# Two triangular inverses under way at once in a chunked recurrence

## The chip, the cores and the metric

The kernel runs on one core of a Trainium2 chip. The metric is the device time of one execution in microseconds (us), the median of three runs. Lower is better.

## The reference, cut to what matters

The reference is two transformer blocks over 1024 tokens of width 1024, all in float32. The change touches one part of the second block's first layer, the RWKV-7 time mix: 12 heads of 64 channels, with a state of 64 x 64 per head that is carried from token to token.

```python
def step(state, inp):
    r_t, w_t, k_t, v_t, kk_t, a_t = inp
    sa = jnp.einsum('bhvk,bhk->bhv', state, -kk_t)
    state = (state * w_t[:, :, None, :]
             + sa[..., None] * (kk_t * a_t)[:, :, None, :]
             + v_t[..., None] * k_t[:, :, None, :])
    y_t = jnp.einsum('bhvk,bhk->bhv', state, r_t)
    return state, y_t
```

## The kernel before, in words

Everything ahead of the recurrence and behind it (the projections, the attentions, the feed-forward) is one long list of steps, each of which issues its instructions on the engines. The recurrence is one step of that list, the class `Rwkv`, between two joins at which all engines wait for each other.

The 1024 tokens are cut into 16 chunks of 64 (`NCH`, `CH`). Inside a chunk the token-by-token update is replaced by matrix products of 64 x 64 per head and by the inverse of a unit lower triangular 64 x 64 matrix per head. The 12 heads lie as 6 pairs; a product for all heads (`heads`, L2281 and on) is 12 matmuls, one per head, and its result fills one PSUM bank, which one instruction of 128 x 384 then reads. A float32 matmul is two instructions in the trace, a float16 one is one.

The work of a chunk is cut into five parts, each a Python generator for every engine, which issues a few instructions between two `yield`s:

- L (`low_rank_*`, 4 steps, for two chunks at a time, so at every second chunk): the decay and rate projections; PE multiplies, DVE adds a bias, ACT takes tanh, and DVE scales the rate (L2321).
- E (`elementwise_*`, 4 steps): step 1 is DVE's decay (L2380) and its running sum, a scan (L2382), and ACT's two exponentials of it (L2361, L2364); step 2 is DVE's three products for the keys and POOL's two behind them (L2347, L2349); step 3 is DVE's L2395, L2396, L2399 and POOL's L2352; step 4 is a PE sum and DVE's bonus (L2403).
- P (`products_*`, 4 steps): step 1 is PE's three products (two of them 128 wide), DVE's masks of them (L2448 to L2460), ACT's cast to float16 (L2493) and POOL's copies and masks; steps 2 to 4 each turn one operand on PE and copy it out of PSUM on ACT (L2499).
- I (`inverse_*`, 12 steps): the inverse by doubling. For each of five levels one step for w (PE product in float16, DVE mask L2538), then one for x (two PE products, DVE additions L2541 and L2543 into `x16` and `xt16`). Step 11 is a refinement in float32: ACT casts `xt16` to `z` (L2560), PE multiplies, DVE subtracts (L2547). Step 12 multiplies once more and adds (L2552).
- S (`state_*`, 4 steps): the state. PE product, ACT copy `rhs` (L2604); PE product, ACT copy `g` (L2607); PE product of the addition; PE product of the output, ACT copy (L2611), DVE's state addition and decay (L2621, L2623).

Each engine runs its instructions strictly in the order in which they were issued and waits for the others by semaphores. That order is set by `order()`, a text of letters written by hand. `run_parts` goes through it on every engine alike: each letter advances that part's generator by a step. In the kernel before, during the states S of chunk m the letters mean: P and I of chunk m+1, E and L of chunk m+2. All 12 steps of a chunk's inverse fall inside the one turn of the loop. There is one set of buffers for the inverse (`low`, `z`, `zi`, `x16`, `xt16`, `w16`, `l16`), and it uses banks 4 (w and the refinement), 5 (x) and 6 (xt); bank 7 serves L, E and the turned operands; banks 0 to 3 serve P, S and half of L.

Of the kernel before, what the change touches and what calls it, by code (L numbers as in the profile page):

```python
# [2171 lines left out]
class Rwkv(Step):  # L2172
# [4 lines left out]
    def __init__(self, k, rkv, lora, rooms):  # L2177
# [17 lines left out]
        self.low, self.z, self.zi = buf(), buf(), buf()  # L2195
        self.x16, self.xt16, self.w16, self.l16 = (buf(BT, CH, dtype=F16) for _ in range(4))
# [20 lines left out]
    def order(self):  # L2217

        out = [("L", 0)] * 4 + [("E", 0)] * 4
        out += [("P", 0)] * 4 + [("I", 0)] * 12 + [("E", 1)] * 4  # L2220
        for m in range(NCH):
            text = ("P L IP L IP L IP L I E I S E I I E S I E I S I I S I" if m % 2 == 0 else
                    "P IP IP IP E I I E I S E I S I E I S I I S I")
            text = "S S S S" if m == NCH - 1 else "P IP IP IP I S I I S I I S I I S I" if m == NCH - 2 else text
            chunk = {"P": m + 1, "I": m + 1, "S": m, "E": m + 2, "L": m + 2}
            count = {c: text.count(c) for c in "PIESL"}
            out += [(c, chunk[c]) for c in text.replace(" ", "")]
            if m < NCH - 1:
# [81 lines left out]

    def low_rank_dve(self, dve, m):
        k, s = self.k, self.s
        for dst, to, bias in (("tw", self.tw, k.vec["a_w0_2"]), ("ta", self.ta, k.vec["a_a0_2"])):
            for half, b in ((0, 7), (1, 0 if dst == "tw" else 1)):
# [55 lines left out]
    def elementwise_dve(self, dve, m):  # L2370
# [32 lines left out]
        dve.scalar_tensor_tensor(vC, self.bank(7), 64.0, self.vc, ALU.mult, ALU.mult).then_inc(*s.bonus.up(m))  # L2403
        yield

    def elementwise_pe(self, pe, m):
        k, s = self.k, self.s
        yield
        yield
        yield  # L2410
        pe.wait_ge(*self.freed(7))
        pe.wait_ge(*s.e_rk.at(m))
        pe.matmul(self.bank(7), k.block64, self.rk.rearrange("p a b -> p (a b)"), start=True, stop=True).then_inc(*s.e_sum.up(m))
        k.free[7] = ("bonus", m)
        yield

    def products_pe(self, pe, m):
# [7 lines left out]
        pe.wait_ge(*self.freed(4))  # L2425
        self.heads(pe, 4, BT, CH, [(self.ar_e[:, :, 0, :], self.bb)]).then_inc(*s.p_low.up(m))
        k.free[4] = ("low", m)
# [6 lines left out]
        for n, src in enumerate((self.vc, self.kb, self.bb)):  # L2434
            if n == 0:
                pe.wait_ge(*s.e_vc.at(m))
            pe.wait_ge(*self.freed(7))
            self.heads(pe, 7, BT, CH, [(src, over_pairs(k.eye))]).then_inc(*s.p_turn.up((m, n)))
            k.free[7] = ("turned_bkv", (m, n))
            yield  # L2440

    def products_dve(self, dve, m):
# [8 lines left out]
        dve.tensor_tensor(self.low, self.bank(4), over_pairs(k.low), ALU.mult).then_inc(*s.low.up(m))  # L2451
        dve.wait_ge(*s.low.at(m))
        if m:
            dve.wait_ge(*s.inv_z.at(m - 1))
        dve.tensor_tensor(self.z, self.low, over_pairs(k.level[0]), ALU.mult).then_inc(*s.step_dve.up(("z", m)))
        dve.wait_ge(*s.step_dve.at(("z", m)))
        dve.tensor_tensor(self.x16, self.z, over_pairs(k.eye), ALU.add).then_inc(*s.inv_x.up((m, 0)))
# [8 lines left out]
    def products_pool(self, pool, m):  # L2466
# [10 lines left out]
        if m:  # L2477
            pool.wait_ge(*s.inv.at(m - 1))
        pool.tensor_tensor(self.zi, self.lr[i][:, :, 0:CH], over_pairs(k.level0t), ALU.mult).then_inc(*s.step_pool.up(("zi", m)))
        pool.wait_ge(*s.step_pool.at(("zi", m)))  # L2480
        pool.tensor_tensor(self.xt16, self.zi, over_pairs(k.eye), ALU.add).then_inc(*s.inv_xt0.up(m))
# [5 lines left out]
    def products_act(self, act, m):  # L2487
# [3 lines left out]
        if m:  # L2491
            act.wait_ge(*s.inv.at(m - 1))
        act.copy(self.l16, self.lr[i][:, :, 0:CH]).then_inc(*s.inv_l.up(m))  # L2493
# [3 lines left out]
        for n, dst in enumerate((self.vt[i], self.kt[i], self.bt[i])):  # L2497
            act.wait_ge(*s.p_turn.at((m, n)))
            act.copy(dst, self.bank(7)).then_inc(*s.turned_bkv.up((m, n)))  # L2499
            yield  # L2500

    def inverse_pe(self, pe, m):
        k, s = self.k, self.s
        for lev in range(1, 6):
# [3 lines left out]
            pe.wait_ge(*self.freed(4))  # L2508
            self.heads(pe, 4, BT, CH, [(self.l16, self.x16)]).then_inc(*s.i_w.up((m, lev)))
            k.free[4] = ("inv_w", (m, lev))  # L2510
            yield
            pe.wait_ge(*self.freed(5))
            pe.wait_ge(*self.freed(6))
# [17 lines left out]
        k.free[5] = ("inv", m)
        yield

    def inverse_dve(self, dve, m):
        k, s = self.k, self.s
        for lev in range(1, 6):
            dve.wait_ge(*s.i_w.at((m, lev)))
            dve.tensor_tensor(self.w16, self.bank(4), over_pairs(k.level[lev]), ALU.mult).then_inc(*s.inv_w.up((m, lev)))  # L2538
            yield
            dve.wait_ge(*s.i_x.at((m, lev)))  # L2540
            dve.tensor_tensor(self.x16, self.x16, self.bank(5), ALU.add).then_inc(*s.inv_x.up((m, lev)))  # L2541
            dve.wait_ge(*s.i_xt.at((m, lev)))
            dve.tensor_tensor(self.xt16, self.xt16, self.bank(6), ALU.add).then_inc(*s.inv_xt.up((m, lev)))  # L2543
# [3 lines left out]
        dve.tensor_tensor(self.r16, self.bank(4), self.zi, ALU.subtract).then_inc(*s.inv_rest.up(m))  # L2547
# [4 lines left out]
        dve.tensor_tensor(self.xt[m % 2], self.z, self.bank(5), ALU.add).then_inc(*s.inv.up(m))  # L2552
        yield

    def inverse_act(self, act, m):
        s = self.s
# [3 lines left out]
        act.copy(self.z, self.xt16).then_inc(*s.inv_z.up(m))  # L2560
# [3 lines left out]
    def inverse_pool(self, pool, m):  # L2564
        s = self.s
# [3 lines left out]
        pool.tensor_tensor(self.zi, self.xt16, over_pairs(self.k.eye), ALU.subtract).then_inc(*s.inv_zi.up(m))  # L2569
# [536 lines left out]
def layer_a(k):  # L3106
# [29 lines left out]
    rwkv = Rwkv(k, (r, key, v), lora, ((k.XH, k.CONST), (F + 6144, F + 8192)))  # L3136
# [3 lines left out]
    yield from [Join(k), RwkvSetup(k, rwkv), KeyNorms(k, key, rwkv.sqs, rwkv.rs12), Join(k), Reset(k, rwkv.reset), rwkv, end]  # L3140
    stored = [(f"dma_stage{j}", main[j - 2].id) for j in range(2)]
# [217 lines left out]
```

## Time and profile before

| what | us |
|---|---|
| median of three runs (3339.84 to 3344.09) | 3340.28 |
| the profiled execution | 3336.7 |
| its span in the profile | 3334.5 |
| recurrence in the span, first heads product to last | 1943.4 to 2415.7 |
| mean granted TensorE clock, share of full | 0.936 |

The page's busy shares over the whole span are PE 86%, DVE 51%, ACT 30% and POOL 21%. They average over stages with quite different limits, so for this change the reader has to look at the recurrence alone, which is a seventh of the span. The profiled execution's own time is 2.2 us above its span. A row of the timeline gives the start of an instruction, or of a run of like ones, its duration, and in brackets how long the engine was idle before it and which instruction released it. Instructions of DVE that follow each other without a wait overlap at their ends: 128 x 384 elements last 0.55 us but start 0.47 us apart.

### The profile page before, as it was taken

To read this page: it belongs to the slowest core of one execution; us is meant where nothing else is said; L and a number is where in the kernel's file an instruction comes from. 1 tells how busy PE (TensorE), PEld (TensorE's weight loads), DVE (VectorE), ACT (ScalarE), POOL (GpSimd) and SP (SyncE) were. 2 spreads that over 40 slices of the span, in tenths; PEclk is the share of its full clock that TensorE was granted. 3 is DMA by queue.
4 is the path that set the end of the run, shared out by engine and by line. 5 is a ranking of instruction groups with operands and counts; after the bars stand their busy time and mean duration, and the time that the engine had idled before them with its cause. 6 is when DMAs were issued, how large, how long until landed. Compare 5 with 4: busy or idle time off the path is not lost.

```text
span 3334.5 us, 49994 instructions
## 1 busy us (share of the span) xinstructions
PE 2870.6 (86%) x20746; PEld 2301.4 (69%) x20746; DVE 1707.7 (51%) x3034; ACT 985.6 (30%) x1803; POOL 686.1 (21%) x531
## 2 busy tenths in 40 slices
PE   7998878799999999689999867777758899999767
PEld 6776666588888888467788546666627678766545
DVE  3426555444444444675554167677654433377634
ACT  3224444311111111633221211211143222255543
POOL 2112234211101010252111022222112211122123
PEclk8999999899999999899999968989879899999978
DMA  3120032111111111022112100000032201101222
GB/s 103 48 63 26 14 108 70 32 51 39 57 45 51 39 57 53 30 82 82 39 39 69 44 1 3 3 3 3 3 114 76 95 26 40 38 31 37 86 76 76
DMA packets 196449, 162.45 MB, mean 49 GB/s; under 512 B 5200, under 2 KB 173818, under 8 KB 195458
## 3 DMA queue, kind: packets, MB, share of 16 engines
q1 hardware_dynamic: 196226, 159.26, 15.3%
q8 instruction: 166, 2.72, 0.3%
q14 instruction: 57, 0.47, 0.0%
HBM read 137.19 MB, written 22.05 MB: 48 GB/s over the span
## 4 chain that ended last, share of the span: by engine, by line
PE 71%; DVE 16%; ACT 6%; issue 4%; POOL 2%; DMA 1%; SPq 0%; DVEq 0%; ACTq 0%; POOLq 0%
PE ps L725 15%; PE ps L726 15%; PE ps L727 15%; PE ps L2290 5%; PE ps L1840 3%; PE ps L1764 2%; PE ps L1466 2%; DVE r L690 2%; PE ps L1468 1%; PE ps L1467 1%; ACT r L685 1%; PE ps L777 1%; PE ps L1831 1%; PE ps L779 1%; PE ps L778 1%
## 5 line engine op out<-in xcount | busy, mean ns | idle before, releaser
L725 PE MATMUL ps<-r,r 128*128 128x512 f32 (+1 forms) x2304 | 942.4, 409 | 144.3 <-DVE r L690 117.4
L726 PE MATMUL ps<-r,r 128*128 128x512 f32 (+1 forms) x2304 | 914.4, 397 | 0.0
L727 PE MATMUL ps<-r,r 128*128 128x512 f32 (+1 forms) x2304 | 913.4, 396 | 0.0
L725 PEld LDWEIGHTS ps<-r,r 128*128 128x128 f32 x2304 | 446.1, 194 | 279.2 <-DVE r L690 130.4
L671 POOL TENSOR_TENSOR sb<-sb 128x1024 f32<-128x1024 f32 x138 | 280.4, 2037 | 1306.7 <-DMA sb<-in_w_ffn_up 483.7
L726 PEld LDWEIGHTS ps<-r,r 128*128 128x128 f32 x2304 | 446.9, 194 | 93.6 <-issue 5.9
L727 PEld LDWEIGHTS ps<-r,r 128*128 128x128 f32 x2304 | 445.2, 193 | 95.7
L2290 PE MATMUL ps<-sb 64*64 64x64 f32 (+2 forms) x8832 | 300.9, 226 | 121.9 <-DVE sb L2541 29.8
L2290 PEld LDWEIGHTS ps<-sb 64*64 64x64 f32 (+1 forms) x8832 | 280.2, 136 | 151.0 <-issue 99.1
L690 DVE TENSOR_TENSOR r<-sb,r 128x1024 fp32r<-128x1024 f32 x198 | 267.4, 1358 | 190.0 <-ACT r L685 189.8
L685 ACT CAST r<-sb 128x1024 fp32r<-128x1024 f32 x198 | 204.8, 1043 | 213.1 <-POOL sb L671 213.0
L1840 PE MATMUL ps<-sb 128*128 128x64 f32 (+1 forms) x1008 | 140.4, 284 | 21.7 <-ACT sb L1853 17.1
L1840 PEld LDWEIGHTS ps<-sb 128*128 128x128 f32 x1008 | 128.0, 197 | 41.0 <-issue 21.6
L930 DVE TENSOR_TENSOR sb<-sb 128x512 f32<-128x512 f32 x70 | 62.0, 885 | 165.6 <-ACT sb L920 154.1
L1466 PE MATMUL ps<-r,r 128*128 128x512 f32 x352 | 138.6, 394 | 8.4 <-DVE sb L1479 7.8
L1418 ACT CAST r<-sb 128x512 fp32r<-128x512 f32 x44 | 27.3, 620 | 384.9 <-DVE sb L1433 384.9
L1468 PE MATMUL ps<-r,r 128*128 128x512 f32 x352 | 137.1, 389 | 0.0
L1467 PE MATMUL ps<-r,r 128*128 128x512 f32 x352 | 137.0, 389 | 0.0
L1479 DVE TENSOR_TENSOR sb<-sb,ps 128x512 f32<-128x512 f32 x160 | 106.0, 684 | 54.6 <-PE ps L1468 54.6
L1782 DVE CUSTOM_DVE_ANT_0 sb<-ps,sb 128x128 f32<-128x128 f32 (+7 forms) x160 | 121.0, 756 | 21.7 <-PE ps L1764 20.2
L1795 ACT ACTIVATE sb<-sb 128x128 f32<-128x128 f32 (+7 forms) x160 | 123.1, 772 | 25.9 <-DVE sb L1785 25.4
L1764 PE MATMUL ps<-sb 64*128 64x512 f32 (+2 forms) x480 | 103.6, 537 | 4.0 <-DVE sb L1782 1.8
(276 smaller groups left out, 3606.8 us busy)
## 6 DMA issues: line engine op xcount, KB each, us to landing
sb<-in_w_out SPq DMA_DIRECT2D x36, 512.0 KB, 4.0
sb<-in_a_w_in SPq DMA_DIRECT2D x29, 512.0 KB, 4.0
sb<-in_w_ffn_gate SPq DMA_DIRECT2D x22, 512.0 KB, 3.9
sb<-in_w_ffn_up SPq DMA_DIRECT2D x22, 512.0 KB, 3.8
sb<-in_w_ffn_down SPq DMA_DIRECT2D x22, 512.0 KB, 3.4
sb<-in_w_in SPq DMA_DIRECT2D x17, 512.0 KB, 4.1
sb<-in_x SPq DMA_DIRECT2D x16, 512.0 KB, 5.6
xs<-sb SPq DMA_DIRECT2D x4, 2048.0 KB, 9.6
```

Source lines behind the costliest of these rows:

```text
L671: pool.tensor_tensor(w.raw, w.raw, w.gain.unsqueeze(2).broadcast_to((P, w.nk, w.n)), ALU.mult).then_inc(*s.w_gain.up(w.id))
L685: act.copy(w.hi, w.raw).then_inc(*s.w_hi.up(w.id))
L690: dve.tensor_tensor(w.lo, w.raw, w.hi.bitcast(F32), ALU.subtract).then_inc(*s.w_lo.up(w.id))
L725: pe.matmul(self.out, w.hi[:, q, self.cols], hi, start=(q == 0), stop=False)
L726: pe.matmul(self.out, w.hi[:, q, self.cols], lo, start=False, stop=False)
L727: ins = pe.matmul(self.out, w.lo[:, q, self.cols], hi, start=False, stop=(q == w.nk - 1))
L1466: pe.matmul(self.out, w.hi[:, 0, cols], hi, start=(q == 0), stop=False)
L1467: pe.matmul(self.out, w.hi[:, 0, cols], lo, start=False, stop=False)
L1468: ins = pe.matmul(self.out, w.lo[:, 0, cols], hi, start=False, stop=(q == 1))
L1764: ins = pe.matmul(k.banks(2 * h)[:, b:b + m], of.q(i)[o, iq * P:(iq + 1) * P], of.keys(i)[o, b:b + m], start=True, stop=True)
L1840: ins = pe.matmul(k.ps[:, b, o], of.pt[:, g % 2, j * P:(j + 1) * P], of.v(i, first + j)[:, o], start=(first + j == 0), stop=(first + j == ...
L2290: ins = pe.matmul(self.bank(b + p // n, n, w)[o, p % n, :], lhs[o, p], rhs[o, p], start=(j == 0), stop=(j == len(pairs) - 1), skip_group_c ...
```

## The change

The inverse of chunk m+1 and that of chunk m+2 are now both under way in one turn of the loop. In the new text A stands for the second half of chunk m+1's inverse (steps 7 to 12), B for the first half of chunk m+2's (steps 1 to 6); P is that of chunk m+2, E and L are those of chunk m+3. One text serves even and odd chunks; L is left out where its chunk is odd. The inverse's seven buffers exist twice, taken by the chunk's parity, in a third room of SBUF whose last use is the staging of the gates (hence a wait on two stores ahead of the recurrence). Each of the two inverses has two banks, 4 and 5 or 6 and 7: x goes into w's bank. What bank 7 held moves to banks 0, 1 and 3. The number and the sizes of the compute instructions stay as they were.

```diff
-        self.low, self.z, self.zi = buf(), buf(), buf()
-        self.x16, self.xt16, self.w16, self.l16 = (buf(BT, CH, dtype=F16) for _ in range(4))
+        self.low, self.z, self.zi = ([buf() for _ in range(2)] for _ in range(3))
+        self.x16, self.xt16, self.w16, self.l16 = ([buf(BT, CH, dtype=F16) for _ in range(2)] for _ in range(4))
...
     def order(self):
-        out = [("L", 0)] * 4 + [("E", 0)] * 4
-        out += [("P", 0)] * 4 + [("I", 0)] * 12 + [("E", 1)] * 4
+        out = [("L", 0)] * 4 + [("E", 0)] * 4 + [("P", 0)] * 4 + [("E", 1)] * 4 + [("I", 0)] * 2 + [("L", 2)] * 4
+        out += [step for _ in range(4) for step in (("P", 1), ("I", 0))]
+        out += [step for _ in range(4) for step in (("I", 0), ("E", 2), ("I", 1))] + [("I", 0)] + [("I", 1)] + [("I", 0)] + [("I", 1)]
         for m in range(NCH):
-            text = ("P L IP L IP L IP L I E I S E I I E S I E I S I I S I" if m % 2 == 0 else
-                    "P IP IP IP E I I E I S E I S I E I S I I S I")
-            text = "S S S S" if m == NCH - 1 else "P IP IP IP I S I I S I I S I I S I" if m == NCH - 2 else text
-            chunk = {"P": m + 1, "I": m + 1, "S": m, "E": m + 2, "L": m + 2}
...
+            chunk = {"S": m, "A": m + 1, "P": m + 2, "B": m + 2, "E": m + 3, "L": m + 3}
+            for c in "S A S A S S P A P B L A P L B L E P A L B E A B E B E B".split():
+                if chunk[c] < NCH and (c != "L" or chunk[c] % 2 == 0):
+                    out.append(("I" if c in "AB" else c, chunk[c]))
...
     low_rank_pe, low_rank_dve
-            for half, b in ((0, 7), (1, 0 if dst == "tw" else 1)):
+            for half, b in ((0, 0), (1, 1)):
...
     products_pe
-            pe.wait_ge(*self.freed(7))
-            self.heads(pe, 7, BT, CH, [(src, over_pairs(k.eye))]).then_inc(*s.p_turn.up((m, n)))
-            k.free[7] = ("turned_bkv", (m, n))
+            pe.wait_ge(*self.freed(n % 2))
+            self.heads(pe, n % 2, BT, CH, [(src, over_pairs(k.eye))]).then_inc(*s.p_turn.up((m, n)))
+            k.free[n % 2] = ("turned_bkv", (m, n))
...
     inverse_pe
+        b, bt = 4 + 2 * i, 5 + 2 * i
-            self.heads(pe, 4, BT, CH, [(self.l16, self.x16)]).then_inc(*s.i_w.up((m, lev)))
+            self.heads(pe, b, BT, CH, [(self.l16[i], x16)]).then_inc(*s.i_w.up((m, lev)))
...
-            self.heads(pe, 5, BT, CH, [(self.xt16, self.w16)]).then_inc(*s.i_x.up((m, lev)))
-            self.heads(pe, 6, BT, CH, [(self.w16, self.xt16)]).then_inc(*s.i_xt.up((m, lev)))
+            self.heads(pe, b, BT, CH, [(xt16, w16)]).then_inc(*s.i_x.up((m, lev)))
+            self.heads(pe, bt, BT, CH, [(w16, xt16)]).then_inc(*s.i_xt.up((m, lev)))
...
     layer_a
-    rwkv = Rwkv(k, (r, key, v), lora, ((k.XH, k.CONST), (F + 6144, F + 8192)))
+    rwkv = Rwkv(k, (r, key, v), lora, ((k.XH, k.CONST), (F + 6144, F + 8192), (F + 14336, F + 16384)))
+    stored = [(f"dma_stage{j}", main[j - 2].id) for j in range(2)]
```

How the order moves is best seen where a turn without L meets ACT. First ACT's instructions of such a turn in the kernel before, from the mask's cast (L2493) to the next turn's (the semaphore each waits for is in brackets; the two exponentials are L2361 and L2364, the cast to `z` is L2560):

```order
L2493 CAST sb<-sb 128x384 [waits s_inv,s_lr]
L2499 COPY sb<-ps 128x384 [waits s_p_turn,s_s_y]
L2499 COPY sb<-ps 128x384 [waits s_p_turn] x2
L2361 ACTIVATE sb<-sb 128x6x64 [waits s_ar_copied,s_e_run]
L2364 ACTIVATE sb<-sb 128x384 [waits s_e_kb]
L2604 COPY sb<-ps 128x384 [waits s_s_rhs]
L2607 COPY sb<-ps 128x384 [waits s_s_g]
L2560 CAST sb<-sb 128x384 [waits s_inv_xt]
L2611 COPY sb<-ps 128x6x64 [waits s_s_y]
```

Then the same turn on ACT in the changed kernel, where the lines have shifted (mask's cast L2489, turned operands L2495, exponentials L2358 and L2361, cast to `z` L2559, state copies L2603, L2606, L2610):

```order
L2603 COPY sb<-ps 128x384 [waits s_s_rhs]
L2606 COPY sb<-ps 128x384 [waits s_s_g]
L2610 COPY sb<-ps 128x6x64 [waits s_s_y]
L2489 CAST sb<-sb 128x384 [waits s_inv,s_lr]
L2495 COPY sb<-ps 128x384 [waits s_p_turn,s_s_y]
L2495 COPY sb<-ps 128x384 [waits s_p_turn]
L2358 ACTIVATE sb<-sb 128x6x64 [waits s_ar_copied,s_e_run]
L2361 ACTIVATE sb<-sb 128x384 [waits s_e_kb]
L2495 COPY sb<-ps 128x384 [waits s_p_turn]
L2559 CAST sb<-sb 128x384 [waits s_inv_xt]
```

The three state copies have come together at the head of the turn, and the third turned operand and the cast to `z` now stand directly behind the two exponentials, which wait for DVE's scan.

The same place on DVE in the changed kernel, from the scan (printed here as SCALAR_TENSOR_TENSOR, L2379) to the last instruction of the turn's E, B and bonus (L2546 subtracts in step 11 and was L2547; L2537 is the mask of w and was L2538; L2540 and L2542 are the additions of x and were L2541 and L2543; L2551 ends the inverse and was L2552):

```order
L2379 SCALAR_TENSOR_TENSOR sb<-sb 128x384 [waits s_step_dve]
L2546 TENSOR_TENSOR sb<-ps,sb 128x384 [waits s_inv_zi,s_i_rest]
L2537 TENSOR_TENSOR sb<-ps,sb 128x384 [waits s_i_w]
L2383 SCALAR_TENSOR_TENSOR sb<-sb 128x384 [waits s_rate]
L2385 SCALAR_TENSOR_TENSOR sb<-sb 128x384 [waits s_step_dve]
L2386 SCALAR_TENSOR_TENSOR sb<-sb 128x384
L2551 TENSOR_TENSOR sb<-sb,ps 128x384 [waits s_s_y,s_i_fix]
L2540 TENSOR_TENSOR sb<-sb,ps 128x384 [waits s_i_x]
L2542 TENSOR_TENSOR sb<-sb,ps 128x384 [waits s_i_xt]
L2392 TENSOR_TENSOR sb<-sb 128x6x64 [waits s_e_pc,s_ar_copied,s_turned_bkv]
L2393 TENSOR_TENSOR sb<-sb 128x6x64
L2396 TENSOR_TENSOR sb<-sb 128x384 [waits s_e_nb,s_e_pinv]
```

Behind the scan DVE now has the subtraction of step 11 as its very next instruction; before, the w mask of a level or the key products of E stood there.

## Rows read from the trace of the kernel before

**Rows 1.** Busy time by stretch: the whole recurrence, then two chunks of it.

```profile
core 0: us, PE busy (x) PEld busy (x) DVE busy (x) ACT busy (x) POOL busy (x), PEclk, DMA share, GB/s
1944.00:2415.70 471.70, 340.38 (x9026) 308.27 (x9024) 325.82 (x592) 89.51 (x185) 114.06 (x139) 0.90 0.01 3
2059.00:2118.00 59.00, 44.00 (x1142) 39.96 (x1138) 41.76 (x78) 11.56 (x24) 14.75 (x18) 0.88 0.01 3
```

**Rows 2.** DVE's state addition (L2621), sixteen in all, then single ones in time.

```profile
L2621 DVE TENSOR_TENSOR sb<-sb,ps x16: 553/555/555, 2007.0 to 2416.1; 128x384 f32<-128x384 f32 x16
...
2124.01 0.55 DVE L2621 TENSOR_TENSOR sb<-sb,ps 128x384 f32<-128x384 f32 x1 [1.61 <-PE ps L2290]
...
2150.76 0.55 DVE L2621 TENSOR_TENSOR sb<-sb,ps 128x384 f32<-128x384 f32 x1 [1.61 <-PE ps L2290]
...
2181.12 0.56 DVE L2621 TENSOR_TENSOR sb<-sb,ps 128x384 f32<-128x384 f32 x1 [1.61 <-PE ps L2290]
...
2382.49 0.56 DVE L2621 TENSOR_TENSOR sb<-sb,ps 128x384 f32<-128x384 f32 x1 [1.61 <-PE ps L2290]
```

**Rows 3.** DVE in order of time: start, duration, line, tiles, idle before it.

```profile
1931.59 0.56 DVE L2317 TENSOR_TENSOR sb<-ps,sb 128x384 f32<-128x384 f32 x1 [0.92 <-PE ps L2305]
...
1949.74 0.54 DVE L2460 TENSOR_TENSOR sb<-ps,sb 128x384 f32<-128x384 f32 x1
...
2066.60 0.55 DVE L2448 TENSOR_TENSOR sb<-ps,sb 128x384 f32<-128x384 f32 x1
...
2070.97 0.54 DVE L2538 TENSOR_TENSOR sb<-ps,sb 128x384 f16<-128x384 f32 x1
...
2080.53 1.20 DVE L2395 TENSOR_TENSOR sb<-sb 128x384 f32<-128x384 f32 x1
...
2083.26 0.55 DVE L2538 TENSOR_TENSOR sb<-ps,sb 128x384 f16<-128x384 f32 x1
...
2084.47 0.55 DVE L2541 TENSOR_TENSOR sb<-sb,ps 128x384 f16<-128x384 f16 x1 [0.67 <-PE ps L2290]
...
2084.95 0.55 DVE L2543 TENSOR_TENSOR sb<-sb,ps 128x384 f16<-128x384 f16 x1
...
2110.04 0.96 DVE L2382 TENSOR_TENSOR_SCAN sb<-sb 128x384 f32<-128x384 f32 x1
...
2110.92 0.53 DVE L2538 TENSOR_TENSOR sb<-ps,sb 128x384 f16<-128x384 f32 x1
...
2114.39 0.63 DVE L2395 TENSOR_TENSOR sb<-sb 128x384 f32<-128x384 f32 x1
```

**Rows 4.** PE in order of time, runs of matmuls merged.

```profile
1964.60 1.54 PE L2290 MATMUL ps<-sb 64*64 64x64 f32 x24 [1.42 <-ACT sb L2560]
...
2084.06 0.56 PE L2290 MATMUL ps<-sb 64*64 64x64 f16 x24 [0.66 <-DVE sb L2538]
...
2089.14 6.57 PE L2290 MATMUL ps<-sb 64*64 64x64 f32 x180 [1.56 <-ACT sb L2560]
...
2097.40 0.38 PE L2290 MATMUL ps<-sb 64*64 64x64 f16 x12 [0.83 <-issue]
...
2410.74 0.92 PE L2290 MATMUL ps<-sb 64*64 64x64 f32 x24 [0.61 <-issue]
...
2412.23 3.71 PE L2290 MATMUL ps<-sb 64*64 64x64 f32 x120 [0.57 <-ACT sb L2607]
```

**Rows 5.** ACT in order of time.

```profile
2076.49 0.53 ACT L2361 ACTIVATE sb<-sb 128x384 f32<-128x384 f32 x1
...
2076.91 0.51 ACT L2364 ACTIVATE sb<-sb 128x384 f32<-128x384 f32 x1
...
2088.48 0.51 ACT L2560 CAST sb<-sb 128x384 f32<-128x384 f16 x1 [4.56 <-DVE sb L2543]
```

**Rows 6.** POOL in order of time.

```profile
2079.30 1.11 POOL L2347 TENSOR_TENSOR sb<-sb 128x384 f32<-128x384 f32 x1 [2.14 <-DVE sb L2388]
```

**Rows 7.** Page, DMA issues: KB each, us from issue to landing.

```profile
xs<-sb SPq DMA_DIRECT2D x4, 2048.0 KB, 9.6
```

More of the change, by code:

```diff
@@ L2313, in low_rank_dve @@
         for dst, to, bias in (("tw", self.tw, k.vec["a_w0_2"]), ("ta", self.ta, k.vec["a_a0_2"])):
-            for half, b in ((0, 7), (1, 0 if dst == "tw" else 1)):
+            for half, b in ((0, 0), (1, 1)):
                 pairs = slice(3 * half, 3 * half + 3)
@@ L2402, in elementwise_dve @@
         dve.wait_ge(*s.e_vc.at(m))
-        dve.scalar_tensor_tensor(vC, self.bank(7), 64.0, self.vc, ALU.mult, ALU.mult).then_inc(*s.bonus.up(m))
+        dve.scalar_tensor_tensor(vC, self.bank(3), 64.0, self.vc, ALU.mult, ALU.mult).then_inc(*s.bonus.up(m))
         yield
@@ L2410, in elementwise_pe @@
         yield
-        pe.wait_ge(*self.freed(7))
+        pe.wait_ge(*self.freed(3))
         pe.wait_ge(*s.e_rk.at(m))
-        pe.matmul(self.bank(7), k.block64, self.rk.rearrange("p a b -> p (a b)"), start=True, stop=True).then_inc(*s.e_sum.up(m))
-        k.free[7] = ("bonus", m)
+        pe.matmul(self.bank(3), k.block64, self.rk.rearrange("p a b -> p (a b)"), start=True, stop=True).then_inc(*s.e_sum.up(m))
+        k.free[3] = ("bonus", m)
         yield
@@ L2424, in products_pe @@
         k.free[0] = k.free[1] = ("lr", m)
[L2425 to L2427 removed]
+        b = 4 + 2 * (m % 2)
+        pe.wait_ge(*self.freed(b))
+        self.heads(pe, b, BT, CH, [(self.ar_e[:, :, 0, :], self.bb)]).then_inc(*s.p_low.up(m))
+        k.free[b] = ("low", m)
         pe.wait_ge(*s.e_kb.at(m))
@@ L2490, in products_act @@
         act.wait_ge(*s.lr.at(m))
-        if m:
-            act.wait_ge(*s.inv.at(m - 1))
-        act.copy(self.l16, self.lr[i][:, :, 0:CH]).then_inc(*s.inv_l.up(m))
+        if m > 1:
+            act.wait_ge(*s.inv.at(m - 2))
+        act.copy(self.l16[i], self.lr[i][:, :, 0:CH]).then_inc(*s.inv_l.up(m))
         yield
@@ L2498, in products_act @@
             act.wait_ge(*s.p_turn.at((m, n)))
-            act.copy(dst, self.bank(7)).then_inc(*s.turned_bkv.up((m, n)))
+            act.copy(dst, self.bank(n % 2)).then_inc(*s.turned_bkv.up((m, n)))
             yield
     def inverse_pe(self, pe, m):
-        k, s = self.k, self.s
+        k, s, i = self.k, self.s, m % 2
+        b, bt = 4 + 2 * i, 5 + 2 * i
+        x16, xt16, w16 = self.x16[i], self.xt16[i], self.w16[i]
         for lev in range(1, 6):
@@ L2546, in inverse_dve @@
         dve.wait_ge(*s.inv_zi.at(m))
-        dve.tensor_tensor(self.r16, self.bank(4), self.zi, ALU.subtract).then_inc(*s.inv_rest.up(m))
+        dve.tensor_tensor(self.r16[i], self.bank(b), self.zi[i], ALU.subtract).then_inc(*s.inv_rest.up(m))
         yield
@@ L2551, in inverse_dve @@
             dve.wait_ge(*s.s_y.at(m - 2))
-        dve.tensor_tensor(self.xt[m % 2], self.z, self.bank(5), ALU.add).then_inc(*s.inv.up(m))
+        dve.tensor_tensor(self.xt[i], self.z[i], self.bank(bt), ALU.add).then_inc(*s.inv.up(m))
         yield
     def inverse_act(self, act, m):
-        s = self.s
+        s, i = self.s, m % 2
         for _ in range(10):
@@ L2559, in inverse_act @@
         act.wait_ge(*s.inv_xt.at((m, 5)))
-        act.copy(self.z, self.xt16).then_inc(*s.inv_z.up(m))
+        act.copy(self.z[i], self.xt16[i]).then_inc(*s.inv_z.up(m))
         yield
@@ L2568, in inverse_pool @@
         pool.wait_ge(*s.inv_xt.at((m, 5)))
-        pool.tensor_tensor(self.zi, self.xt16, over_pairs(self.k.eye), ALU.subtract).then_inc(*s.inv_zi.up(m))
+        pool.tensor_tensor(self.zi[i], self.xt16[i], over_pairs(self.k.eye), ALU.subtract).then_inc(*s.inv_zi.up(m))
         yield
@@ L3139, in layer_a @@
     end.fills_ring = True
-    yield from [Join(k), RwkvSetup(k, rwkv), KeyNorms(k, key, rwkv.sqs, rwkv.rs12), Join(k), Reset(k, rwkv.reset), rwkv, end]
-    stored = [(f"dma_stage{j}", main[j - 2].id) for j in range(2)]
+    yield from [Join(k), RwkvSetup(k, rwkv), KeyNorms(k, key, rwkv.sqs, rwkv.rs12), Join(k),
+                After(k, act=stored, dve=stored, pool=stored), Reset(k, rwkv.reset), rwkv, end]
     yield from finish_layer(k, 0, stored, HeadNorm(k, r, v, F))
```

55 lines of the change are left out of this document (24 added, 31 removed).

## The prediction

> **What bounds the recurrence now.** I read the share of busy time by stretch first. In the 471.7 us of the recurrence DVE is busy 326 us and PE 340 us [rows 1]; neither is saturated, and PE's busy time holds the tails of short runs. DMA moves 3 GB/s, so it plays no part. ACT is busy 90 us and POOL 114 us: they matter only by when they act. So this stage is bound by waits between PE and DVE, which is what a second inverse could fill. Then I took the sixteen state additions [rows 2] as a clock of the loop: the first at 2007.0, the last at 2416.1. Thirteen periods up to 2382.49 take 375.5 us, 28.9 us each; seven are turns without L, six with L. The pair from 2124.01 to 2181.12 takes 57.1 us, of which the turn without L, to 2150.76, is 26.8 and the one with L 30.3. Last, the timelines by engine [rows 3 to 6] give the price of each step, and I walk one turn of the new order with them.
>
> **Prices.** DVE: back to back, instructions of 128 x 384 start 0.47 apart and end 0.55 after their start [rows 3]. Step 1 of P takes DVE 4.4 (2066.60 to 2070.97). Step 1 of E is 0.38 plus 0.88 for the scan, 1.26 in all (2110.04 to 2110.92 is the scan). Step 2 of E is 1.5, three instructions of which the second waits for the first. Step 3 of E was 2.7 in one chunk (2080.53 to 2083.26) and about 2.2 where its first multiply took 0.63 (2114.39); I take 2.5. PE: 12 float16 matmuls (x12) deliver after 0.38, 24 (both products of x) after 0.56, so 12 occupy PE 0.18 and their result is 0.2 late; 24 float32 instructions deliver after 0.92 and occupy 0.70; the 120 of addition and output deliver after 3.71; the run of 180 that ends in P's three products takes 6.57 [rows 4], from which the 24 wide ones of one product come out at 1.33. From a state product over its ACT copy to the next state product is 1.49 (2410.74 to 2412.23) [rows 4]. DVE's mask of w ends at 2083.81 and PE's x starts at 2084.06, 0.25 later; DVE adds x 0.41 after that start [rows 3, 4]. ACT: the exponentials start 0.42 apart; the cast to `z` starts at 2088.48 and PE's refinement at 2089.14, 0.66 later [rows 4, 5].
>
> **A turn without L in the new order.** Zero is the end of DVE's mask in the last w of B. What follows on DVE is 19.6 us of work: bonus 0.5, B's x 0.9, A's first w and x 1.4, state 1.1, P 4.4, then w of A and of B and both x 2.8, scan 1.3, subtraction and w 0.9, E's step 2 1.5, last addition 0.5, x 0.9, E's step 3 2.5, w 0.5, and some 0.4 of rounding and of waits for own results. The waits in it:
> - PE does x of B until 0.62, then the first state product (1.40) and only then A's w. DVE waits 0.3 for the x of B and 0.8 for that w.
> - The state product is ready at 2.24, ACT's copy lets the next start at 2.85, A's x is issued behind it at 3.55: DVE waits 1.0.
> - After ACT's second copy the addition and output start at 4.34 and reach DVE at 8.17. DVE has had nothing since 4.87: 3.3. Before, steps of the inverse stood between the state's products; two of them do now, where four or five did.
> - P's first product comes from PE at 9.38: 0.15. Two x later in the turn: 0.4.
> - At about 17 DVE starts the scan and ends it at 18.3. Next on DVE is the subtraction of A's step 11. It needs PE's refinement, which needs ACT's cast to `z`. `xt16` has been ready since 16.0, but on ACT the two exponentials and the third turned operand stand ahead of the cast, and the exponentials need the scan. So: exponentials 0.84, turned copy 0.4, cast and hand-over 0.66, product 0.92, small hand-overs: the subtraction starts at 21.1. DVE stands idle 2.9.
> The waits sum to 8.9 and the turn to 28.5 us. Before, such a turn takes 26.8 [rows 2].
>
> **A turn with L.** To 28.5 it adds four biases (0.47 each) and two scalings (0.36 each), 2.6, and these waits: L's second half now needs bank 1, which ACT frees only after it has copied a turned operand (1.3 on DVE); two scalings wait for ACT's tanh (0.6 each, as before, but with less put between); the last half of L is issued behind the refinement (0.3). Less 0.6 of waits that fall away. That makes 33.3, where 30.3 stood [rows 2].
>
> Thirteen turns, seven without L and six with: 199.5 + 199.8 = 399.3 us. These prices are from stretches in which the clock was full. Before, thirteen fast turns would be 6 x 57.1 and one short of 26.8, 369.4; the trace has 375.5, so 6.1 go to a lower clock, as where 24 float32 instructions took 1.54 in place of 0.92 [rows 4]. I carry 6.1 over: 405.4, which is **+29.9** against 375.5.
>
> **The ends.** Start: P of chunk 0 ends on DVE at 1950.2 [rows 3]. Before, I of chunk 0 follows alone, PE and DVE in turn, then E. Now E of chunk 1 (5.7 with its waits) and two steps of I (1.5) come first, L of chunk 2 (5.4, as the first L took from 1931.59 to the start of E), P of chunk 1 (5.2), then ten steps of I between P's and E's (17.5): the first turn's zero is at about 1986.7, its state addition at 1994.9 instead of 2007.0: **-12.1**. Tail: from the fourteenth addition to the last took 33.6. Now it is a turn of 22.0 without E and 13.6 more for the bare state chain: 35.6, **+2.0**. The wait for two stores of gates ahead of the recurrence I set at nothing: two joins and the key norms stand between their issue and the wait, and a 2 MB store, far larger than these, lands in 9.6 us [rows 7], which bounds it if that cover were gone. The doubled buffers take away waits of ACT and POOL on the previous inverse that were not the last to end.
>
> Sum: +29.9 - 12.1 + 2.0 = **+19.8 us**. On the profiled execution's 3336.7 us that is 3356.5; the median of the runs lay 3.6 above that execution, and the forecast for the median is 3340.3 + 19.8 = **3360 us**. A measurement can tell about 0.2%, 6.7 us, from no change. It needs an average turn of 29.7 us (375.5 + 10.1, over 13) to come out even; my walk has 30.7, or 31.2 with the clock.
>
> **Two prices that are open.** E's step 3 runs while POOL forms its two products (1.11 for the first) [rows 6]. DVE's multiply took 1.20 with POOL at work and 0.63 at another time [rows 3]; all three multiplies slow would be 3.4, all fast 1.6, so -0.9 to +0.9 a turn, -12 to +12 us; I take the middle since POOL's two products end part way through. The Trainium skill (SBUF — State Buffer, Who interferes with whom) says that of a DVE instruction with two SBUF inputs and a GpSimd one that reads SBUF, the second blocks until the first is done; by that rule the upper end holds wherever POOL is busy, and the time would be nearer 3372. The other is the handling of several waits on one instruction: between 0.05 and 0.25 a step [rows 3, 4], on about ten hand-overs of a turn that end DVE's waits, so -1 to +1 a turn at most; I use each step's own row.
>
> **Rivals.**
> - *The second inverse fills the waits* (faster). DVE's work is 19.6 and 22.2 a turn. The mechanism would be that ACT's cast to `z` runs as soon as `xt16` is there, during the scan, so that PE's refinement is done when DVE asks for it; then up to 2.9 a turn goes, 38 us: 3360 - 38 = 3322. For it: the sum of DVE and PE idle time that is there [rows 1]. Against it: the order on ACT, which no speed changes. It decides from 29.1 us a turn down. Chance 0.13.
> - *It comes out even*: the walk is 1 to 2 us a turn too high, from small overlaps that it misses: 3334 to 3347. Chance 0.15.
> - *The clock falls more often* (slower still). PE now stands idle some 3.5 us before each refinement. In the trace PE's gap ahead of the refinement was 1.56 us [rows 4] and the clock of the loop 0.88 to 0.90 of full [rows 1]; the stretch with 1.54 for a 0.92 run [rows 4] was the single inverse at the start, where PE did little. At 1.2 GHz a run of 24 float32 instructions takes 0.62 more (1.54 for 0.92); two or three such runs on the path of each turn cost 1.2 to 1.9, 16 to 25 in all: about 3380. The Trainium skill (TensorE: Matmul & The Clock Gate, HAM oscillation — how this bites in real kernels) says that matmul bursts with long waits between them bring the engine back to half its clock at every burst; the time by it would be this rival's. Chance 0.10.
> - *The forecast*, slower by 7 to 30 us, 3347 to 3370: 0.62.
> That two inverses are not really in flight is no case: the order shows both on every engine.
>
> So faster 0.13, same 0.15, slower 0.72. The range holds the forecast, the even case and most of the open prices, and reaches to the third rival's middle; what it leaves out is most of the first rival and the far half of the third, under 0.2 together: 3330 to 3380.
>
> **What would show it.** Right: in the changed profile a turn of DVE shows one wait near 3 us before the state addition and one near 3 us before L2546, released by PE; ACT's L2559 starts within 1 us behind L2495, which follows L2361; periods between state additions (L2620) of about 28 and 33 us; the first of them some 12 us earlier than before. Wrong: periods under 27 and 31, or L2546 without a wait, or a PEclk of the loop under 0.85 (then the clock, and not the order, sets the size).

## The result and the profile after

| what | before | after |
|---|---|---|
| median, us | 3340.5 (4 runs beside after's) | 3387.39 (4 runs, 3385.24 to 3389.49) |
| profiled execution and its span | 3336.7, 3334.5 | 3385.2, 3384.0 |
| mean granted TensorE clock of the span | 0.936 | 0.917 |

The change makes the kernel **slower by 47 us**: the ratio is 1.0138, 95% interval 1.0121 to 1.0156. The direction is the predicted one; the time lies 7 us above the range and 27 above the forecast.

The same order of reading as before. First the share by stretch of after: the row that answers to [rows 1], then one turn without L in steps of 3 us.

```profile
core 0: us, PE busy (x) PEld busy (x) DVE busy (x) ACT busy (x) POOL busy (x), PEclk, DMA share, GB/s
1944.00:2416.00 472.00, 335.72 (x7985) 300.18 (x7987) 308.18 (x557) 80.72 (x171) 114.46 (x136) 0.78 0.01 2
...
2139.00:2142.00 3.00, 2.40 (x96) 2.29 (x96) 2.87 (x7) 0.48 (x1) 0.00 (x0) 1.00 0.00 0
2142.00:2145.00 3.00, 0.10 (x2) 0.13 (x4) 0.98 (x2) 1.71 (x4) 0.59 (x2) 0.99 0.00 0
2145.00:2148.00 3.00, 2.58 (x63) 2.47 (x65) 1.49 (x3) 0.00 (x0) 0.79 (x1) 0.50 0.02 5
2148.00:2151.00 3.00, 1.18 (x30) 0.97 (x26) 3.00 (x7) 0.00 (x0) 2.28 (x3) 0.50 0.00 0
...
2154.00:2157.00 3.00, 3.00 (x64) 2.90 (x60) 0.83 (x2) 0.25 (x1) 0.00 (x0) 0.50 0.03 5
...
2160.00:2163.00 3.00, 3.00 (x108) 3.00 (x106) 0.04 (x1) 0.00 (x0) 0.00 (x0) 1.00 0.03 5
```

The granted clock of the recurrence is 0.78, against 0.90 in [rows 1]. In one turn it stands at full until 2145, is at half (1.2 instead of 2.4 GHz) for some 13 us, and comes back in the dense run of the state. Ahead of the fall PE did almost nothing for 3 us (0.10 of 3.00 busy).

Then the loop's clock, the state additions (L2620), which answer to [rows 2]: first of the turn shown and the next.

```profile
2132.80 0.55 DVE L2620 TENSOR_TENSOR sb<-sb,ps 128x384 f32<-128x384 f32 x1 [3.16 <-PE ps L2287]
...
2163.19 0.55 DVE L2620 TENSOR_TENSOR sb<-sb,ps 128x384 f32<-128x384 f32 x1 [3.16 <-PE ps L2287]
```

The first addition of all stands at 2001.54, the fourteenth at 2425.49, the last at 2464.37. So thirteen periods take 423.95 us, 32.6 each; those without L 29.2 to 30.4, those with L 35.0 to 36.2.

Who waits, DVE's groups over the recurrence, of before and then of after (engine and line that waits, for whom, us in total, times, longest):

```profile
DVE sb L2541 <- PE ps L2290: 32.7, 41, 2.1
DVE sb L2621 <- PE ps L2290: 30.8, 16, 6.9
DVE sb L2317 <- PE ps L2305: 29.8, 21, 2.8
DVE sb L2547 <- PE ps L2290: 26.0, 16, 2.3
...
DVE sb L2538 <- PE ps L2290: 9.9, 15, 1.7
```

```profile
DVE sb L2620 <- PE ps L2287: 57.0, 16, 10.1
DVE sb L2546 <- PE ps L2287: 46.7, 16, 3.5
DVE sb L2537 <- PE ps L2287: 30.8, 15, 2.2
DVE sb L2540 <- PE ps L2287: 24.2, 35, 1.6
DVE sb L2314 <- PE ps L2302: 14.7, 15, 1.1
```

The state addition waits 26 us more, the subtraction of step 11 (L2547 before, L2546 after) 21 more, the mask of w (L2538, L2537) 21 more; the additions of x (L2541, L2540) 9 less and L's biases (L2317, L2314) 15 less. Together that is 44 of the 49.5 by which the two spans differ. Two of the three large new waits were in the prediction. The third, the mask of w, is one row in the turn of after:

```profile
2142.05 0.96 DVE L2379 TENSOR_TENSOR_SCAN sb<-sb 128x384 f32<-128x384 f32 x1
2146.48 0.56 DVE L2546 TENSOR_TENSOR sb<-ps,sb 128x384 f16<-128x384 f32 x1 [3.47 <-PE ps L2287]
...
2157.07 0.56 DVE L2537 TENSOR_TENSOR sb<-ps,sb 128x384 f16<-128x384 f32 x1 [2.23 <-PE ps L2287]
2159.02 0.55 DVE L2540 TENSOR_TENSOR sb<-sb,ps 128x384 f16<-128x384 f16 x1 [1.39 <-PE ps L2287]
```

ACT and PE in the same turn of after, in order of time:

```profile
2143.05 0.52 ACT L2358 ACTIVATE sb<-sb 128x384 f32<-128x384 f32 x1 [2.03 <-DVE sb L2379]
...
2143.89 0.46 ACT L2495 COPY sb<-ps 128x384 f32<-128x384 f32 x1
2144.24 0.51 ACT L2559 CAST sb<-sb 128x384 f32<-128x384 f16 x1
```

```profile
2144.90 1.86 PE L2287 MATMUL ps<-sb 64*64 64x64 f32 x36 [3.29 <-ACT sb L2559]
...
2153.25 3.78 PE L2287 MATMUL ps<-sb 64*64 64x64 f16 x84 [0.83 <-issue]
```

ACT is the queue that the prediction described: the cast to `z` (L2559) starts 1.2 us behind the first exponential, and PE has stood idle 3.29 us. The last row is the new thing: the run of 84 holds the x of B, the first state product and A's w. It lasts 3.78 us at half clock, and DVE's waits of 2.23 and 1.39 hang on it and on its successor.

### The profile page after: what moved, and what is told of

Same layout as the page of the kernel before. It is cut to its first block, busy times and chain, and to the rows that moved or that the text cites. A ratio compares the mean times of both kernels' runs of the same rounds, so it can differ in the third digit from the quotient of the medians.

```text
span 3384.0 us, 49900 instructions
## 1 busy us (share of the span) xinstructions
PE 2906.8 (86%) x20746; PEld 2331.3 (69%) x20746; DVE 1704.6 (50%) x3034; ACT 983.2 (29%) x1803; POOL 685.3 (20%) x531
## 4 chain that ended last, share of the span: by engine, by line
PE 71%; DVE 13%; ACT 7%; issue 5%; POOL 3%; DMA 2%; SPq 0%; DVEq 0%; ACTq 0%; POOLq 0%
PE ps L725 15%; PE ps L726 14%; PE ps L727 14%; PE ps L2287 7%; PE ps L1840 3%; PE ps L1764 3%; DVE r L690 1%; PE ps L1466 1%; PE ps L1831 1%; ACT r L685 1%; PE ps L1467 1%; PE ps L1468 1%; PE ps L777 1%; PE ps L779 1%; PE ps L778 1%
## 5 line engine op out<-in xcount | busy, mean ns | idle before, releaser
L2287 PE MATMUL ps<-sb 64*64 64x64 f32 (+2 forms) x8832 | 318.0, 236 | 135.3 <-issue 52.9
L2287 PEld LDWEIGHTS ps<-sb 64*64 64x64 f32 (+1 forms) x8832 | 301.5, 145 | 169.0 <-issue 130.7
```

The costliest lines, as they stand in the source:

```text
L2287: ins = pe.matmul(self.bank(b + p // n, n, w)[o, p % n, :], lhs[o, p], rhs[o, p], start=(j == 0), stop=(j == len(pairs) - 1), skip_group_c ...
```

## The experiments

**The exponentials out of the cast's way.** In after, ACT's part of E issues its two exponentials one step later, so that the cast to `z` stands ahead of them.

```diff
     def elementwise_act(self, act, m):
         s = self.s
+        yield
...
         act.activation(self.pinv, self.run, ACT.Exp, scale=-1.0).then_inc(*s.e_pinv.up(m))
-        yield
```

> The changed kernel with one thing moved: ACT issues the two exponentials of E in step 2 of E in place of step 1, so the third turned operand's copy and the cast to z stand ahead of them; PE, DVE and POOL keep their order. Theory 1 (ACT's order makes DVE wait at the subtraction of step 11, and the long pause of PE that goes with it brings the clock down for the rest of the turn): DVE's wait there falls from 2.9 us to about 1, which is 13 x 2 = 26 us off 3387, and the clock of the loop rises above 0.85 and takes up to 18 us more: 3343 to 3361. Theory 2 (the low clock has nothing to do with that pause): 3361, clock as in the changed kernel. Theory 3 (the wait is the price of the refinement itself, not of ACT's order): within 5 us of 3387.

Measured: 3361.91 us, ratio to before 1.0068 (1.0053 to 1.0083), 25.5 less than after. ACT of this kernel, then DVE's waits:

```profile
2137.93 0.52 ACT L2559 CAST sb<-sb 128x384 f32<-128x384 f16 x1
2138.35 0.53 ACT L2359 ACTIVATE sb<-sb 128x384 f32<-128x384 f32 x1
```

```profile
DVE sb L2620 <- PE ps L2287: 57.2, 16, 9.5
DVE sb L2537 <- PE ps L2287: 31.1, 16, 2.2
...
DVE sb L2546 <- PE ps L2287: 15.0, 8, 2.3
DVE sb L2546 <- POOL sb L2568: 10.2, 8, 1.3
```

The subtraction's wait falls from 46.7 to 25.2 us, and the total falls by about as much. Ten of what is left now end with POOL's subtraction (L2568): with PE early, POOL is late next. The two other waits have not moved at all. PE's pause ahead of the refinement is down from some 3.2 us to 1.08, and yet the granted clock over 2000 to 2300 us is 0.83, where after has 0.79: of what was expected, the second theory came nearest, in which the pause of PE is not what keeps the clock low. So the order on ACT is one part of the loss, and it is worth 25 us, not the 38 that the first rival set on it.

**PE kept at work ahead of the refinement.** In after, PE is given 144 idle float16 matmuls, idle because nothing reads their results: they go into the bank that the refinement then overwrites.

```diff
         pe.wait_ge(*self.freed(b))
+        for _ in range(12):
+            self.heads(pe, b, BT, CH, [(self.l16[i], x16)])
         pe.wait_ge(*s.inv_z.at(m))
```

> The changed kernel with 144 float16 matmuls of 64 x 64 added on PE ahead of each refinement, where PE waits for ACT's cast; their results are overwritten by the refinement's product. They last about 2.2 us at full clock and no wait is taken away. Theory 1 (the pause of PE lowers the clock, which costs about 1.4 us a turn): the clock stays near full in E's part of the turn, turns fall from 32.6 to about 31.2, 3369. Theory 2 (the clock falls for another reason, or costs nothing): 3387 or up to 10 us more.

Measured: 3380.01 us, ratio 1.0123 (1.0108 to 1.0138), only 7.4 less than after. One turn of it in steps of 3 us, and PE's run with the state product:

```profile
2142.00:2145.00 3.00, 1.18 (x50) 0.93 (x42) 2.79 (x6) 0.00 (x0) 0.73 (x2) 1.00 0.00 0
2145.00:2148.00 3.00, 1.26 (x14) 0.59 (x14) 3.00 (x6) 0.00 (x0) 2.42 (x3) 0.96 0.03 5
2148.00:2151.00 3.00, 2.05 (x51) 2.08 (x52) 2.33 (x5) 0.00 (x0) 0.00 (x0) 0.50 0.00 0
```

```profile
2148.95 3.78 PE L2287 MATMUL ps<-sb 64*64 64x64 f16 x84 [1.56 <-issue]
```

The pause ahead of the refinement is gone, and the clock stays full to 2148. Then it falls all the same, behind two stretches in which DVE works through E and PE is busy 1.2 of 3 us; the run of 84 still takes 3.78. (The subtraction of step 11 still waits 2.89 here, now for POOL's L2570.) So the pause that the prediction's third rival named is not the only place that costs the clock. Here it fell behind E's part of the turn, in which PE has little to do, and that lies right ahead of the state. The 3369 us of the first theory were not reached: the thirteen periods take 414.40 us here, 9.6 less than in after, of which the last two turns give 2.7 back.

**PE kept at work in E's part instead.** In after, 96 idle matmuls behind the x of level 2 and 36 behind E's sum, into the other inverse's bank.

```diff
+            if lev == 2 and m > 2:
+                other = 4 + 2 * ((m + 1) % 2)
+                pe.wait_ge(*self.freed(other))
+                for _ in range(8):
+                    self.heads(pe, other, BT, CH, [(self.l16[i], self.l16[i])])
             yield
...
         k.free[3] = ("bonus", m)
+        if m > 3:
+            other = 4 + 2 * (m % 2)
+            pe.wait_ge(*self.freed(other))
+            for _ in range(3):
+                self.heads(pe, other, BT, CH, [(self.l16[(m + 1) % 2], self.l16[(m + 1) % 2])])
```

> After, with PE given idle products to do where it has little real work: 96 float16 matmuls behind the x of level 2 and 36 behind E's sum, all into the other inverse's free bank, whose results nobody reads; nothing in the output changes. Theory 1 (E's part of the turn leaves PE so little to do that its granted clock falls to 0.50 there, and the state product that follows then runs at half clock): the granted clock of the loop, 0.79 over 2000 to 2300 us in after, rises above 0.92, the run of 84 instructions with the state product in it goes from 3.78 to about 2.2, DVE's wait before the first w mask from 2.23 to about 0.8, a turn loses 1.4 to 2.2 us and the whole lands at 3387.4 minus 18 to 29, 3358 to 3370, which is where the walk of the prediction had it without the clock. Theory 2 (the clock costs nothing on the path, the turn is longer because the order is): 3382 or more. Theory 3 (the added matmuls hold up the real ones): over 3390.

Measured: 3374.46 us, ratio 1.0088 (1.0066 to 1.0109), 12.9 less than after (15 less if each is set against the kernel before as it was measured beside it, 3342.63 and 3340.5). That is 4 us above what the first theory had. Its loop and the stretch ahead of a state product, the first w of the turn that ends at 2130.67 with the state additions behind it (here L2630):

```profile
2000.00:2300.00 300.00, 225.91 (x6502) 208.27 (x6495) 198.37 (x362) 54.60 (x117) 70.15 (x85) 0.88 0.01 3
...
2121.00:2124.00 3.00, 2.86 (x93) 2.19 (x95) 2.95 (x6) 0.00 (x0) 0.26 (x1) 0.96 0.02 5
```

```profile
2124.93 0.56 DVE L2547 TENSOR_TENSOR sb<-ps,sb 128x384 f16<-128x384 f32 x1 [0.79 <-PE ps L2287]
...
2130.67 0.55 DVE L2630 TENSOR_TENSOR sb<-sb,ps 128x384 f32<-128x384 f32 x1 [3.19 <-PE ps L2287]
...
2159.10 0.56 DVE L2630 TENSOR_TENSOR sb<-sb,ps 128x384 f32<-128x384 f32 x1 [3.16 <-PE ps L2287]
```

With the clock full where the state product runs, DVE waits 0.79 us for that w, where the walk had 0.8; the turn without L is 28.4 us long (2130.67 to 2159.10), where the walk had 28.5, and the turn with L behind it 34.1 (to 2193.19), where it had 33.3. Over the loop the turns without L take 28.4 to 30.0, those with L 34.0 to 34.7. Thirteen periods are 407.05 us, the prediction's 405.4 within 2, and 16.9 less than after's. The total gained less, in part because the last two turns took 43.1 instead of 38.9: there DVE waits for a w that stands behind the idle matmuls on PE, where the same mask (L2537) in after starts at 2439.01 with a wait of 0.10.

```profile
2428.71 0.56 DVE L2547 TENSOR_TENSOR sb<-ps,sb 128x384 f16<-128x384 f32 x1 [2.71 <-PE ps L2287]
```

So the missing 17 us of the loop were the clock. The loop's granted clock, 0.88, did not reach the 0.92 that was expected, for the pause ahead of the refinement was left in. What counts is where the clock is full and not its mean: the experiment before, with 0.87, gained little more than half as much in the loop.

**Both together.** The edits of the first and the third experiment.

> After with both cures: ACT's two exponentials one step later (as in e1) and PE's idle products in E's part (as in e5). Theory 1 (the two losses, the cast behind the exponentials and the half clock ahead of the state, lie one behind the other on DVE): the savings add up, e1's 25.5 and e5's 18 to 29, so 3333 to 3344, about the kernel before, and what is left over the walk is the wait of 3.2 before each state addition. Theory 2 (they share the same idle time): 3350 or more.

Measured: 3346.68 us, ratio 1.0013 (1.0004 to 1.0023). The thirteen periods are 377.27 us, 17.2 less than with the exponentials alone (394.46), which is again what the idle matmuls gave by themselves. The savings add up: the cast and the clock ahead of the state are two separate losses. The total is 3 us above what was expected, for the tail again (42.4, where the exponentials alone had 39.4). Its longest wait on DVE shows what remains:

```profile
DVE sb L2630 <- PE ps L2287: 55.3, 16, 8.0
```

The state addition still waits as long as in after; what holds it is where the state's products stand. That the whole is back at before all the same is because L's biases and the additions of x wait some 30 less than there. No run moved the state's products and nothing else, so what their place costs by itself is read from this wait and not measured.

**The old order with the new buffers.** After's buffers, banks and room, with before's text of letters and before's prologue.

```diff
-            chunk = {"S": m, "A": m + 1, "P": m + 2, "B": m + 2, "E": m + 3, "L": m + 3}
-            for c in "S A S A S S P A P B L A P L B L E P A L B E A B E B E B".split():
...
+            text = ("P L IP L IP L IP L I E I S E I I E S I E I S I I S I" if m % 2 == 0 else
+                    "P IP IP IP E I I E I S E I S I E I S I I S I")
```

> The changed kernel's buffers and banks (two of everything, L and the turned operands on banks 0 and 1) with the order of the kernel before. Theory 1 (all of the loss comes from the order): 3335 to 3345. Rival (the shared banks 0, 1 and 3 cost): turns with L grow by 1 to 2 us as L waits for ACT's copies, 3350 or more.

Measured: 3339.55 us (10 runs), ratio 1.0000 (0.9988 to 1.0012). The doubled buffers, the other banks and the wait for two stores cost nothing and bring nothing by themselves, within the 4 us of that interval. All of the 47 us is the order. (The loop of the one profiled execution, 3342.29 us, was 6.4 longer than that of before, 381.95 for 375.5: so far apart can single profiles of equally fast kernels lie.)

**A third order, with work between the state's products.** During the states of chunk m, A is the second half of the inverse of chunk m itself, P and B are those of m+1, E and L of m+2. Steps of A, B and E stand between the S, and the two casts of step 11 (`z`, `zi`) are issued one step earlier.

```diff
-            for c in "S A S A S S P A P B L A P L B L E P A L B E A B E B E B".split():
+            chunk = {"S": m, "A": m, "P": m + 1, "B": m + 1, "E": m + 2, "L": m + 2}
+            for c in "P A P B A P L B A L P B L A L E E A S B A S E B S B S E".split():
```

> A third order with the changed kernel's buffers: both inverses one chunk nearer (A is chunk m, P and B chunk m+1, E and L chunk m+2 at state m), seven DVE steps (last addition, three of B, step 3 of E, bonus) stand between the state's products, the casts to z and zi one step earlier. Theory 1 (what counts is what stands on DVE while the state chain and the refinement run): DVE's wait at the state addition falls from 3.2 to under 1 us and that at the subtraction to under 0.5, turns of 24 to 26 us, 3280 to 3305, faster than both kernels. Rival (PE's or ACT's own work sets the turn when DVE is filled): turns of 28 us or more, 3325 or above.

Measured: 3330.83 us (10 runs), ratio to before 0.9977 (0.9967 to 0.9986): 57 us faster than after and just below before. The waits that remain in a turn of it:

```profile
2126.32 0.56 DVE L2538 TENSOR_TENSOR sb<-sb,ps 128x384 f16<-128x384 f16 x1 [2.73 <-PE ps L2285]
...
2129.02 0.56 DVE L2620 TENSOR_TENSOR sb<-sb,ps 128x384 f32<-128x384 f32 x1 [1.69 <-PE ps L2285]
...
2140.77 0.56 DVE L2312 TENSOR_TENSOR sb<-ps,sb 128x384 f32<-128x384 f32 x1 [2.14 <-PE ps L2300]
```

The addition's own wait is down from 3.16 to 1.69, but an x in front of it now waits 2.73 behind the state's long product on PE. The total missed what was expected by 26 us at the least. Turns without L came out at 24.5 to 26.4 us, near the 24 to 26 expected; the miss is in those with L, 30.0 to 31.9, where the biases wait for PE (the third row), and in the last two turns, 45.2 where before had 33.6. Total and mean turn (28.3) lie where the rival had put them, in which PE's own work sets the turn, and the three waits above are all for PE. The x that waits shows besides that a step of I put between two S pays only if its own product doesn't have to queue behind the S.

**The third order, refined.** L runs one chunk further ahead, between the state's products, in banks 6 and 7; E's fourth step (F) moves behind P's first.

```diff
-            for half, b in ((0, 0), (1, 1)):
+            for half, b in ((0, 6), (1, 7)):
...
+            chunk = {"S": m, "A": m, "P": m + 1, "B": m + 1, "F": m + 1, "E": m + 2, "L": m + 3}
+            for c in "P A B F P A B P A B P A E E A S B A S L E B L S B L S L".split():
```

> The order of e4 with two of its remaining waits taken out: L runs a chunk further ahead, between the state's products and in banks 6 and 7, and E's sum and bonus stand behind P's first product. Theory 1 (DVE's waits left in e4, 2.2 and 1.2 for L's banks, 1.4 to 1.75 before the state addition and 0.9 for P's first product, go away where steps of DVE stand in front of them): turns without L 23.6 us (24.5 to 26.1 in e4), with L 27.5 to 28 (30 to 32 in e4), the whole 3295 to 3312. Theory 2 (L's products between the state's products delay the state on PE by as much as they fill): 3325 or more.

Measured: **3297.34 us**, ratio to before 0.9859 (0.9842 to 0.9877): 45 us faster than before (3342.63 beside it) and 90 faster than after, inside what was expected of it. DVE's addition of this kernel at the end of a turn, and its waits in all over the recurrence:

```profile
2205.57 0.55 DVE L2620 TENSOR_TENSOR sb<-sb,ps 128x384 f32<-128x384 f32 x1 [1.38 <-PE ps L2285]
```

```profile
DVE sb L2620 <- PE ps L2285: 23.5, 16, 5.4
```

The state addition waits 23.5 us in all, where before had 30.8 and after 57.0, and the mask of w and the subtraction (3.5 and 3.9 us) hardly at all. Thirteen periods are 344.1 us, 26.5 each. The turns do not differ as expected (23.6 and 28): both kinds stand near 27, with every fourth at 25.5. In this order three of L's four steps stand ahead of a state addition and the fourth behind it, so each turn has a part of L. Of the gain on before, 31 us are in the loop and 14 ahead of the first state addition (1993.19 for 2006.97), while the last two turns lose 5. How much of it is L's place and how much E's fourth step was not taken apart; nor was the same order tried with a single inverse under way.

## Why the prediction came out as it did

By its own steps, against the profiled executions (spans 3384.0 and 3334.5, 49.5 apart, where the sum had +19.8):

| step | predicted | measured |
|---|---|---|
| thirteen turns | +29.9 | +48.4 (423.95 for 375.5) |
| start, counted from L's first product | -12.1 | -9.2 |
| tail, fourteenth addition to last | +2.0 | +5.3 (38.9 for 33.6) |
| stages ahead of and behind the recurrence | 0 | +5.0 |

- **The wait before the state addition**: 3.3 predicted, 3.0 to 3.16 measured in every turn. Right.
- **ACT's queue ahead of the cast to `z`**: 2.9 predicted, 2.9 to 3.5 measured, in the order of instructions that was named. Right, and its removal gives 25.5 us.
- **E's step 3**: 2.5 taken, between 1.6 and 3.4. The three multiplies took 0.73, 1.22 and 0.55, from 2150.34 to the next instruction at 2152.60: 2.26, the same in every turn. The upper end, in which all three are slow beside POOL, did not come, and the time did not go to 3372 by this road. But the rule of the Trainium skill (SBUF — State Buffer, Who interferes with whom), that the second blocks until the first is done, agrees with the trace. The first two multiplies start while a POOL product runs and end 0.41 and 0.42 after that product, the third starts with POOL idle and takes 0.55. The slow one with its POOL product, whose end is at 2151.80:

```profile
2151.00 1.22 DVE L2393 TENSOR_TENSOR sb<-sb 128x384 f32<-128x384 f32 x1
```

```profile
2150.62 1.18 POOL L2349 TENSOR_TENSOR sb<-sb 128x384 f32<-128x384 f32 x1
```

What was off is the range, which let every multiply be slow at once; the price of one follows from when the POOL instruction beside it ends.
- **The banks, the doubled buffers, the two stores**: nothing predicted but 1.3 us for bank 1 in a turn with L, where L's bias waited 1.08; by themselves they cost nothing measurable.
- **The clock: the step that failed.** The prediction had "I carry 6.1 over", the clock loss of the old loop, and gave a loop whose clock falls in every turn 0.10. It falls in every one. The state product's run takes 3.78 us, DVE's wait for A's w is 2.0 to 2.23 instead of 0.8, that for A's x 0.8 to 1.6 instead of 1.0. This is the third rival's mechanism and it came on top of the forecast, at the lower end of its price: 18.5 us over the sum in the loop, 16.9 of which come back when PE is kept at work. Of the tail's 3.3 too much, 2.1 are the same: in the last period the two runs that [rows 4] have at 0.92 and 3.71 took 1.54 and 5.21. The rival was weighed on the length of one pause, 3.5 us against the 1.56 in [rows 4]; what was not looked at is how little PE does in the whole stretch behind it. [rows 1] could not show that, as its stretch is two chunks long. But the trace of before shows it in slices of 3 us, and in the very turn of 26.8 that the prediction took as fast: the clock falls behind E's part, the run of 84 at 2142.75 takes 3.46, and DVE waits for it.

```profile
2139.00:2142.00 3.00, 0.88 (x35) 0.73 (x30) 2.33 (x5) 0.48 (x1) 0.80 (x1) 1.00 0.00 0
2142.00:2145.00 3.00, 3.00 (x56) 2.45 (x58) 1.86 (x4) 0.00 (x0) 0.00 (x0) 0.70 0.03 5
```

```profile
2145.93 0.56 DVE L2541 TENSOR_TENSOR sb<-sb,ps 128x384 f16<-128x384 f16 x1 [2.05 <-PE ps L2290]
```

So the 6.1 were reckoned from turns that had lost clock already, and were too few as the clock's share even of the old loop. The prediction's own sign for this case, a PEclk of the loop under 0.85, is there with 0.78. The text of the Trainium skill that stood beside that rival (TensorE: Matmul & The Clock Gate, HAM oscillation — how this bites in real kernels), bursts with long waits between them bring the half clock back each time, fits the trace of after: 0.50 in every turn, behind a wait of 3.29 us in the turn shown. The second experiment shows that the long wait is not needed: there the clock fell with none above 1.94.
- **The start**: nearly right, with some luck in the sum; the clock of that stretch is 0.73 to 0.78, and the walk's prices were from full clock. The terms that the prediction lists end at 1985.5 and not at its 1986.7, which would have made the start -13.3 and the miss 4 us instead of 3.
- **The stages outside**: 5 us that neither the order nor the recurrence touches. Executions of before alone lie between 3330.5 and 3349.6, so this is within what one profiled execution is off.

## What to carry to other kernels

When a second chain is put in flight, count for each in-order engine what each of its instructions now stands behind, not how much work there is: here ACT and PE were each free enough, and yet DVE stood idle 3 us in every turn for a cast behind two exponentials and 3.16 for a state chain with its products side by side, where the old order had 1.61. Put another chain's steps between the links of the one that is serial, as the refined third order does, and only steps whose own operands are already there. And look at PE in pieces of a few us before pricing a reordering with durations from full clock: a stretch in which another engine works alone can be paid for in the stretch behind it.

## What the runs showed of the hardware

- Idle matmuls paid. 132 float16 matmuls per turn that nobody reads made the loop 16.9 us shorter, since the granted clock in front of the state rose from 0.50 to 0.96 in the turn shown. Where no other engine's work covered them, in the last two turns, they cost 4.
- The clock fell from 1.00 to 0.50 with PE never idle for more than 1.94 us, behind two stretches of 3 us in which it was busy 1.2 each (second experiment).
- A DVE instruction with two inputs in SBUF that starts while a POOL instruction runs takes as long as that one still needs, and 0.41 to 0.42 us more. That holds for all such multiplies and additions of the loop of after (P's two, L2451 and L2453, took 0.86 and 1.23 to 1.24 that way), and beside an idle POOL they take 0.55. A scan takes 0.96 alone and 1.56 where it starts behind a POOL subtraction: in the third order seven scans of the loop do and take 1.55 or 1.56, the other six take 0.96, in one run. The rows are from the refined third order, where the subtraction ends at 2195.34 and the scan 0.82 later. No run took POOL's work away.

```profile
2194.60 1.56 DVE L2377 TENSOR_TENSOR_SCAN sb<-sb 128x384 f32<-128x384 f32 x1
```

```profile
2194.38 0.96 POOL L2567 TENSOR_TENSOR sb<-sb 128x384 f32<-128x384 f16 x1 [8.57 <-DVE sb L2540]
```
